# A decoder-layer kernel whose cached keys and values are cut into six strided tiles and four whole ones instead of eight and two

## The reference

```python
DILATED_BRANCHES = ((128, 1), (512, 4), (2048, 16))

def dilated_attention_sample(q, kc, vc, table, buf_len):
    T = q.shape[1]
    outs, lses = [], []
    for window, dil in DILATED_BRANCHES:
        steps = window // dil
        i = jnp.arange(T)[:, None]
        j = jnp.arange(steps + 1)
        idx = buf_len + i - j[None, :] * dil
        valid = idx >= 0
        idxc = jnp.maximum(idx, 0)
        kg = kc[:, idxc]
        vg = vc[:, idxc]
        bias = rel_bias(table, j * dil)
        s = jnp.einsum('bthd,btjhd->bhtj', q, kg).astype(jnp.float32) * ATT_SCALE + bias[None, :, None, :]
        p, lse = masked_softmax_stats(s, valid[None, None])
        outs.append(jnp.einsum('bhtj,btjhd->bthd', p.astype(vc.dtype), vg))
        lses.append(lse.transpose(0, 2, 1))
    return combine_branches(outs, lses)
```

## Time and profile before

| | us |
|---|---|
| median of three executions | 1987.24 |
| the profiled execution, its own time | 1987.24 |
| its span, first to last instruction | 1985.4 |
| PE busy | 1892.5 (95%) |
| DVE busy | 1051.1 (53%) |
| DMA queue, share of 16 engines | 43.2% |

### The profile page before, as it was taken

The page is one execution under the profiler, slowest core; times in us unless marked ns, Lnnn a source line. Parts: engine busy times, 40 slices in busy tenths (PEclk is TensorE's granted clock), DMA queues, the critical chain, the costliest instruction groups (busy, mean ns, idle before and its releaser), DMA issues.

```text
span 1985.4 us, 33151 instructions
## 1 busy us (share of the span) xinstructions
PE 1892.5 (95%) x13253; PEld 1752.7 (88%) x13253; DVE 1051.1 (53%) x2108; ACT 443.2 (22%) x902; POOL 508.5 (26%) x371
## 2 busy tenths in 40 slices
PE   6999997999999999999999999999999999999987
PEld 6999886677666899999659999999999999999987
DVE  6698726666666553512553464544544544454455
ACT  5100113555555421200540220001000000000005
POOL 2332322010010144453002223233333333223220
PEclk9999998999999999999999999999999999999999
DMA  4399966586777512124531143342342342311102
GB/s 153 131 319 340 330 194 209 161 245 196 210 221 236 186 44 75 54 85 138 191 107 32 42 147 108 127 167 86 126 169 84 126 169 84 127 49 45 43 21 91
DMA packets 220002, 281.36 MB, mean 142 GB/s; under 512 B 7521, under 2 KB 206569, under 8 KB 218153
## 3 DMA queue, kind: packets, MB, share of 16 engines
q1 hardware_dynamic: 219901, 279.94, 43.2%
HBM read 266.48 MB, written 113.89 MB: 192 GB/s over the span
## 4 chain that ended last, share of the span: by engine, by line
PE 81%; DVE 9%; ACT 3%; issue 2%; SPq 2%; DMA 2%; POOL 0%; DVEq 0%; POOLq 0%; ACTq 0%
PE bank L1536 26%; PE bank L1572 12%; PE bank L1303 8%; PE bank L1064 8%; PE bank L1320 4%; PE bank L1182 3%; PE bank L1011 2%; DVE sp L2158 2%; PE bank L1283 2%; PE bank L1155 2%; PE bank L1165 2%; PE bank L1498 1%; PE bank L1210 1%; ACT p_T L1693 1%; PE bank L1122 1%
## 5 line engine op out<-in xcount | busy, mean ns | idle before, releaser
L916 POOL CAST w_hi<-w_raw 128x1024 fp32r<-128x1024 f32 x98 | 104.2, 1063 | 959.4 <-issue 321.9
L1536 PE MATMUL bank<-g_lo,w_hi 128*128 128x362 f32 (+1 forms) x1008 | 333.2, 331 | 0.0
L1536 PE MATMUL bank<-g_hi,w_lo 128*128 128x362 f32 (+1 forms) x1008 | 333.1, 330 | 0.0
L1536 PE MATMUL bank<-g_hi,w_hi 128*128 128x362 f32 (+1 forms) x1008 | 330.5, 328 | 0.0
L918 POOL TENSOR_TENSOR w_lo<-w_raw,w_hi 128x1024 fp32r<-128x1024 f32 x98 | 266.8, 2723 | 7.9
L2566 DVE TENSOR_TENSOR xT<-bank,xT 128x362 f32<-128x362 f32 (+1 forms) x264 | 139.7, 534 | 115.3 <-PE bank L1572 115.3
L1572 PE MATMUL bank<-act_hi,w_hi 128*128 128x364 f32 (+1 forms) x528 | 175.8, 333 | 16.3 <-DVE xT L2566 10.2
L1536 PEld LDWEIGHTS bank<-g_hi,w_lo 128*128 128x128 f32 x1008 | 191.0, 189 | 0.0
L1536 PEld LDWEIGHTS bank<-g_hi,w_hi 128*128 128x128 f32 x1008 | 189.7, 188 | 0.3 <-POOL w_lo L918 0.3
L1536 PEld LDWEIGHTS bank<-g_lo,w_hi 128*128 128x128 f32 x1008 | 189.5, 188 | 0.0
L1572 PE MATMUL bank<-act_lo,w_hi 128*128 128x364 f32 (+1 forms) x528 | 173.9, 329 | 0.0
(11 more groups left out here) (294 smaller groups left out, 3767.8 us busy)
## 6 DMA issues: line engine op xcount, KB each, us to landing
out_sk_dram<-in_cache_win_k_dram SPq DMA_DIRECT2D x24, 2040.0 KB
out_sv_dram<-in_cache_win_v_dram SPq DMA_DIRECT2D x24, 2040.0 KB
kb<-in_cache_win_k_dram SPq DMA_DIRECT2D x48, 512.0 KB, 5.0
vn<-in_cache_win_v_dram SPq DMA_DIRECT2D x22, 1024.0 KB, 8.1
w_raw<-in_w_in_dram SPq DMA_DIRECT2D x22, 512.0 KB, 11.0
w_raw<-in_w_ffn_gate_dram SPq DMA_DIRECT2D x22, 512.0 KB, 3.8
w_raw<-in_w_ffn_up_dram SPq DMA_DIRECT2D x22, 512.0 KB, 3.8
w_raw<-in_w_ffn_down_dram SPq DMA_DIRECT2D x22, 512.0 KB, 3.7
```

What stands on the lines that cost most here:

```text
L916: pool.tensor_copy(w_hi[slot][:, :], w_raw[slot][:, :]).then_inc(w_hi_done, 1)
L1536: last = pe.matmul(out, w, r, start=start, stop=stop)
```

## The change

`FAR, NEAR` goes from 8, 2 to 6, 4. The last 512 rows are now four whole tiles of 128 consecutive rows. The six far tiles hold rows of the first 96 groups: on partitions 0 to 95 row f of each group; on partitions 96 to 127 the rows 6 and 7 of 32 groups at a time (tile f has row 6 + f % 2 of the groups from 32 * (f // 2)). The rows read are the same 1280, and so are the bytes and the 1 KB runs; each row lands in another place. The biases in `d_row` follow in the same order, made by five copies instead of three.

The lots are the same in size: K0 holds far tiles 0 to 3, K1 far tiles 4 and 5 and near tiles 0 and 1, K2 near tiles 2 and 3. The number of DMAs changes: a unit's keys take 6 + 6 + 2 instead of 2 + 2 + 4, and its values 10 instead of 6. The last unit's values take 6 as before, and its early part 6 instead of 2.

```diff
-FAR, NEAR = 8, 2
+FAR, NEAR = 6, 4
 KT = FAR + NEAR
-NEAR0 = BUF - 2 * NEAR * P
+NEAR0 = BUF - NEAR * P
...
-        KEY_DMAS = (2, 2, 4)
-        VALUE_DMAS = 6
+        KEY_DMAS = (6, 6, 2)
+        VALUE_DMAS = 10
...
-            def cached(rows, u, b):
+            def load_far(rows, into, u, f0, f1, arrived):
+
 
                 p, e = divmod(u, 4)
-                row0 = (2 * e + b) * BUF
-                return rows[row0:row0 + BUF, 2 * p * P:(2 * p + 2) * P].rearrange("(g r) c -> g r c", r=16)
-
-            def load_far(rows, into, u, f0, f1, arrived):
-
+                cols = slice(2 * p * P, (2 * p + 2) * P)
                 for b in range(2):
-                    sp_.dma_start(into[:, b, 0:f1 - f0, :], cached(rows, u, b)[:, f0:f1, :]).then_inc(arrived, 16)
-
-            def load_near(rows, into, u, arrived):
-
-                for b in range(2):
-                    for t in range(NEAR):
-                        r0 = FAR + 4 * t
-                        sp_.dma_start(into[:, b, t, :], cached(rows, u, b)[BUF // 16 - 32:BUF // 16, r0:r0 + 4, :])\
-                           .then_inc(arrived, 16)
+                    row0 = (2 * e + b) * BUF
+                    groups = rows[row0:row0 + NEAR0, cols].rearrange("(g r) c -> g r c", r=16)
+                    sp_.dma_start(into[0:96, b, 0:f1 - f0, :], groups[:, f0:f1, :]).then_inc(arrived, 16)
+                groups = rows[2 * e * BUF:(2 * e + 2) * BUF, cols].rearrange("(b g r) c -> g b r c", b=2, r=16)
+                for f in range(f0, f1):
+                    g0 = 32 * (f // 2)
+                    sp_.dma_start(into[96:P, :, f - f0, :], groups[g0:g0 + 32, :, 6 + f % 2, :]).then_inc(arrived, 16)
+
+            def near_tiles(src, u, b, t0, t1):
+                p, e = divmod(u, 4)
+                row0 = (2 * e + b) * BUF + NEAR0
+                return src[row0 + t0 * P:row0 + t1 * P, 2 * p * P:(2 * p + 2) * P]\
+                    .rearrange("(t p) c -> p t c", p=P)
 
             def load_keys(u, j):
                 buf, arrived = kb[(3 * u + j) % 2], kn_in[(3 * u + j) % 2]
                 if j < 2:
-                    load_far(ck_rows, buf, u, 4 * j, 4 * j + 4, arrived)
-                else:
-                    load_near(ck_rows, buf, u, arrived)
+                    load_far(ck_rows, buf, u, 4 * j, 4 + 2 * j, arrived)
+                if j:
+                    for b in range(2):
+                        at, t0 = (2, 0) if j == 1 else (0, 2)
+                        sp_.dma_start(buf[:, b, at:at + 2, :], near_tiles(ck_rows, u, b, t0, t0 + 2)).then_inc(arrived, 16)
...
-                load_near(cv_rows, vn[:, :, FAR:KT, :], u, vn_in)
+                for b in range(2):
+                    sp_.dma_start(vn[:, b, FAR:KT, :], near_tiles(cv_rows, u, b, 0, NEAR)).then_inc(vn_in, 16)
...
-                groups = d_strip[:, BUF + NI - 1:NI - 1:-1].rearrange("p (g r) -> p r g", r=16)
-                pool.tensor_copy(far, groups[:, 0:FAR, :])
-                last_groups = d_strip[:, BUF - NEAR0 + NI - 1:NI - 1:-1].rearrange("p (g r) -> p g r", r=16)
-                for t in range(NEAR):
-                    near = d_row[:, (FAR + t) * P:(FAR + t + 1) * P].rearrange("p (g r) -> p g r", r=4)
-                    last = pool.tensor_copy(near, last_groups[:, :, FAR + 4 * t:FAR + 4 * t + 4])
-                last.then_inc(d_made, 1)
+                groups = d_strip[:, BUF + NI - 1:BUF + NI - 1 - NEAR0:-1].rearrange("p (g r) -> p r g", r=16)
+                pool.tensor_copy(far[:, :, 0:96], groups[:, 0:FAR, :])
+                for q in range(3):
+                    pool.tensor_copy(far[:, 2 * q:2 * q + 2, 96:P], groups[:, 6:8, 32 * q:32 * q + 32])
+                pool.tensor_copy(d_row[:, FAR * P:KT * P], d_strip[:, 7 + NEAR * P:7:-1]).then_inc(d_made, 1)
```

More of the change, by code:

```diff
@@ L1200, in sample_values @@
                 last_unit = u == UNITS - 1
-                pe.wait_ge(vn_in, 16 * VALUE_DMAS * (u + 1))
+                pe.wait_ge(vn_in, 16 * VALUE_DMAS * (u + 1) - (16 * 4 if last_unit else 0))
                 if last_unit:
-                    pe.wait_ge(vn_early_in, 16 * 2)
+                    pe.wait_ge(vn_early_in, 16 * 6)
                 out, full = fill("OS", u)
```

## The result

| | before | after |
|---|---|---|
| median, us | 1987.69 (1987.15 to 1994.3) | 2007.44 (2002.89 to 2012.02) |
| ratio, 95% interval | 1 | 1.0092 [1.0070, 1.0112] |
| profiled execution, us | 1987.24 | 2011.81 |
| its span | 1985.4 | 2010.0 |
| DMA queue, share of 16 engines | 43.2% | 46.4% |

The forecast was 1986.9 us, range 1983.8 to 1991.2. The changed kernel is 19.7 us slower, far outside. The profiled execution of after lies 4.4 us above its own median; the profiles differ by 24.6 us, the medians by 19.7.

What follows compares the result with a forecast made beforehand. Attention was taken as a PE, DVE and ACT chain, with PE waiting for cached keys only twice, in unit 0. 1987.24 + 0.2 (K0(0)) - 0.5 (K2(0)), other terms 0, gave 1986.9 us, range 1983.8 to 1991.2.

Steps and rivals of the forecast that it cites:

- K2(0): Unit 0's third key lot: delay of +0.5 us against a gain of 1.0, together -0.5, range -1.0 to +1.3.
- those 7.3 us: SP's time at the opening spent waiting for room in full DMA queues, claimed to absorb the twelve added issues, 5.6 us.
- K0(0): Unit 0's first key lot, now six issues instead of two: +0.2 us, range 0 to +0.75.
- The gain on two DMAs fewer: K2(0) as two DMAs, not four: first issue to landing 3.46 us instead of 4.47, gain 1.0.
- Both terms go in full into the end: Everything behind the K0(0) and K2(0) waits hangs on PE, so +0.2 and -0.5 us both count fully.
- Later units: Added issues after unit 0 stay hidden, cost 0; unit 10 tightest with 2.1 us spare, range 0 to +0.5.
- POOL's rows: POOL's bias row copies take 2.5 to 3.0 us instead of 2.50; effect 0, range -1.1 to +0.6.
- A: Rival: 32-partition transfers run at half rate, queue stays full longer, +2.6 us, 1989.8; steady units hidden; chance 0.12.
- B: Rival: SP's issue, through a limit on DMAs in flight, becomes the limit; +6.6 to +8.6 us, about 1995; chance 0.08.
- C: Rival: the opening gets shorter and PE keeps its clock, -3.9 us, 1983.3; chance 0.12.
- The signs: Two key waits in unit 0, SP at K2(0) by 339.5 to 341, landing about 3.5 us, share 0.70 to 0.78, POOL 2.5 to 3.0.
- three signs that I had named as refuting: Chain shows a DMA outside unit 0; SP's 22 loads end after 334; 32-partition loads take over 0.60 us to issue.

Runs made afterwards that it cites:

- the cut: Kernel before with each far load of 128 partitions cut into partitions 0 to 95 and 96 to 127: 2011.15 us, ratio 1.0099; cut at 64 instead: 2023.36 us, ratio 1.0163.
- the mixtures: Kernel of DMAs only, no computation, loading blocks of mixed destination shapes, such as values as before and as changed; far loads cut at 96 gave 237 GB/s, at 64 217.

## Why the prediction was wrong

**The step that failed** is in K2(0): "They fit in those 7.3 us: the data set the time of the release, and the data are equal." Its first half held in the main. The second took equal bytes for equal time. I bounded only the 32-partition transfers, at half rate, and left the 96-partition ones, 2.36 MB of a unit's 5.2, at the old 349 GB/s. By the rates measured since, a unit pays

- 2.36 MB x (1/253 - 1/349) = +2.6 us for 96 partitions, forecast 0
- 0.79 MB x (1/196 - 1/349) = +1.8 us for 32 partitions, forecast up to +2.3

4.4 us of the 29.3 that a unit lasts make the share 0.70 + 0.15 = 0.85; the trace has 0.86. With the two corrections named at the cut it would be 0.81, so an agreement to 0.01 is luck; the size is right.

**K0(0)**, forecast +0.2, at most +0.75. From the first issue to the turning 7.19 us (320.04 to 327.23), before 5.77 (321.16 to 326.93): +1.4. Its 0.79 MB into 96 partitions and 0.26 into 32 give by the same rates 0.9 + 0.6 = +1.5. That this fits to 0.1 is luck too: with all loads on 128 partitions the same stretch took 6.54 us with six loads and 6.25 with two, so single profiles differ here by half a us without any slow shape.

**K2(0)**, forecast -0.5. All of the unit's slow transfers stand ahead of it, +4.4 by the rates above; SP reached it +4.2 late. But 1.6 of these came in the same count and order with every load on 128 partitions (20.43 us), where I had forecast 0 to +0.2 by issue; the shapes account for 2.6, less than their rates would give. The gain on two DMAs fewer was real: from first issue to landing 343.55 + 3.22 - 343.10 = 3.67 us, forecast 3.46, before 4.47, so 0.8. Sum 4.2 - 0.8 = +3.4, and by that much PE's turning of K2(0) is late, counted from the stage's first issue: 26.77 us after, 23.40 before. Since after's stage began 1.1 us earlier, +2.3 of it is seen in the end. The +1.4 of K0(0) is not to be added: the later wait swallows it. "Both terms go in full into the end" was a second mistake, a harmless one.

**Later units**, forecast 0, measured +18.2 (20.5 - 2.3). "So they too are absorbed by blocked time" was wrong for the same reason: the blocked time *was* the data's, and these grew. At unit 4 the delay grew by 5.9 and at unit 10 by 10.7, each a wait plus what ran at the lower clock behind it; at unit 8 by 1.6, at full clock, of which 0.94 is the wait and 0.5 a gap of PE ahead of it that the profile puts on no engine (1.68 us instead of 1.15). For unit 10 I had named 2.1 us of spare and up to 1.9 us of added data. Ahead of K2(10) stand 1.97 MB into 96 and 0.66 MB into 32 partitions, 2.1 + 1.5 = 3.6 us by the shapes (4.2 by the mixtures), and 3.5 more came from transfers behind it. Either alone is more than the 2.1.

**POOL's rows**, forecast 0. After, at the opening:

```profile
322.69 1.15 POOL L939 COPY d_row<-d_strip 128x576 f32<-128x576 f32 x1
323.78 0.73 POOL L941 COPY d_row<-d_strip 128x64 f32<-128x64 f32 x3
324.47 0.61 POOL L942 COPY d_row<-d_strip 128x512 f32<-128x512 f32 x1
```

1.15 + 0.73 + 0.61 = 2.49 us, at the low end of my 2.5 to 3.0. Right, and without effect.

**The rivals.** A had the right mechanism at about an eighth of the size (2.6 against 19.7 us), since it gave a lower rate to the 32-partition transfers alone. It called a steady unit hidden, and in eight of them that was so; units 4 and 8 with the strip's loads and unit 10 with the early values were not. B came nearer in time, 1995, for a wrong reason: the 22 loads were out at 331.68, before the 333.8 that was to decide for it, mostly at 0.43 to 0.48 us each, and the same count on full shapes cost no measurable time (0.9988). C never came up: both gaps grew.

**The signs.** K2(0)'s landing, POOL, and the end of the 22 loads came as forecast. SP's arrival at K2(0) (343.1, not 339.5 to 341), the share (0.86, not at most 0.78) and PE's waits (five, not two, with 7.77 and 6.46 us in unit 0) did not. Of the three signs that I had named as refuting, one came: the chain shows a DMA outside unit 0. The other two did not: the 22 loads ended before 334, and ten of the twelve small loads were issued in 0.43 to 0.48 us, the other two in 0.78 and 0.87 with the queue full.

**Still open.** In the stretch of unit 10 the engines moved 216, then 196 and 182 GB/s, where the same shapes alone gave 237 to 257: K2(10) landed at 642.31 instead of 621.0, which is 11.5 us beyond the 9.8 of delay that it came with, and of these some 7 to 7.7 are accounted for. And the last 4.1 us: the cross attention's first turning of cached memory starts 21.6 us later than before, the gate's first 23.1, the last scaling 23.9. In 1100 to 1200 us the granted clock is 0.98 against 1.00, though the two windows hold work shifted by some 22 us; what causes it was not tried.

## What to carry to other kernels

Before a load is cut or laid out anew, count for each DMA how its destination partitions fall on 0 to 63 and 64 to 127; the full rate was seen only at an equal split, and two thirds in one half already cost more than a quarter of the rate. The price of a slower transfer is not paid where it stands but where the next urgent load waits behind it: add up what lies in the queue ahead of each load that has only a few us to spare. And an urgent load belongs ahead of the stores that nobody waits for.

## What the runs showed of the hardware that was not expected

- Sixty-four partitions across the middle (32 to 95) load at 369 GB/s, inside a half at 206 to 207.
- Ninety-six load at 253 to 256. If each half took its own bytes at its own rate, 207 for the fuller one, it would be 207 x 96/64 = 310. So a transfer with an uneven split loses more than its fuller half explains.
- Eight transfers of 64 KB a unit in place of large ones cost no measurable time in this stage (ratio 0.9998 [0.9987, 1.0009]).
- SP's issue mostly takes 0.43 to 0.48 us for 32 and 96 partitions as for 128; with the queue full, single small stores block it for 2.19 and 3.98 us.
- The length of PE's wait alone doesn't tell what clock follows. The transposes behind a wait took 1.09 us (2.4 GHz) after 3.01 us with the far loads on 128 partitions, and after 3.40 us at unit 10 of the changed kernel with K2(0) first. They took 1.97 us (1.2 GHz, granted clock 0.50) after 4.14 us in the changed kernel, but also after 2.61 us at unit 10 of the kernel before cut at 96.
